# The embedding's products between the experts, a weight slot given up for their weights, and results added and normed by pairs of tiles

## What is computed

```python
x = x + merged @ w_o[i]
x = x + hierarchical_moe(rmsnorm(x, g_ffn[i]), ...)        # 32 experts, hidden 256, each token to 2 of them
ple_gate = sigmoid(rmsnorm(x, g_ple[i]) @ w_ple_gate[i])   # 1024 x 1024
x = x + (p[i] @ w_ple[i]) * ple_gate                       # p: 512 x 256, w_ple: 256 x 1024
```

## Time and profile before

| what | value |
|---|---|
| median of three runs | 2403.43 us |
| the profiled execution | 2404.18 us |
| its span in the trace | 2402.3 us |
| mean granted clock of TensorE | 0.988 |
| TensorE busy | 2278.5 us (95%) |
| VectorE busy | 999.4 us (42%) |
| ScalarE busy | 597.6 us (25%) |
| GpSimd busy | 409.7 us (17%) |
| SP's DMA queue, share of the 16 engines' span | 42.6% |

### The profile page before, as it was taken

One profiled execution on the slowest core, in us unless ns is written; L12 is line 12 of the kernel. 1 busy time (PEld: TensorE's weight loads), 2 busy tenths in 40 slices (PEclk: granted clock), 3 DMA queues, 4 the chain that ended last, 5 costly groups with the idle time before them and its releaser, 6 DMA issues. The chain is left out here.

```text
span 2402.3 us, 29837 instructions
## 1 busy us (share of the span) xinstructions
PE 2278.5 (95%) x11892; PEld 1695.5 (71%) x11892; DVE 999.4 (42%) x1787; ACT 597.6 (25%) x1245; POOL 409.7 (17%) x407
## 2 busy tenths in 40 slices
PE   8989999997899989999998889999989999999998
PEld 6666788654458767788754447877768887888887
DVE  6545533511145454543521136445743435232234
ACT  4523401311134443410311125233440003000012
POOL 2011111122211101111122221111101211111111
PEclk9999999999999999999999999999999999999999
DMA  5114536899962112234899982322213332333321
GB/s 172 44 55 107 132 106 261 320 422 422 420 251 61 58 38 70 58 105 164 332 420 422 422 342 64 104 80 86 80 38 101 92 119 73 103 97 97 97 97 71
DMA packets 291930, 396.57 MB, mean 165 GB/s; under 512 B 32590, under 2 KB 232014, under 8 KB 274378
## 3 DMA queue, kind: packets, MB, share of 16 engines
q1 hardware_dynamic: 274880, 366.27, 42.6%
q0 software_dynamic: 11328, 16.81, 1.9%
q10 hardware_dynamic: 5578, 11.51, 1.8%
HBM read 388.98 MB, written 30.15 MB: 174 GB/s over the span
## 5 line engine op out<-in xcount | busy, mean ns | idle before, releaser
L146 PE MATMUL banks<-h_split,w_high 128*128 128x512 f32 (+1 forms) x2640 | 826.8, 395 | 2.8 <-PEq L3441 1.7
L146 PEld LDWEIGHTS banks<-h_split,w_high 128*128 128x128 f32 x2640 | 482.8, 188 | 103.9 <-issue 8.2
L198 DVE TENSOR_TENSOR w_low<-w_raw,w_high 128x1024 fp32r<-128x1024 f32 (+1 forms) x264 | 317.1, 1201 | 506.8 <-POOL w_high L187 506.6
L187 POOL CAST w_high<-w_raw 128x1024 fp32r<-128x1024 f32 (+1 forms) x264 | 276.0, 1046 | 1441.5 <-PE banks L146 1307.3
L146 PE MATMUL banks<-h_split,w_low 128*128 128x512 f32 (+1 forms) x1320 | 513.4, 389 | 0.0
L146 PEld LDWEIGHTS banks<-h_split,w_low 128*128 128x128 f32 x1320 | 247.8, 188 | 52.4
L146 PE MATMUL banks<-w_high,op_split 128*128 128x512 f32 x736 | 228.5, 390 | 1.4 <-DVE mg_part L1420 1.1
L2154 PE MATMUL banks<-expert_ring,ex_xsT 128*64 128x256 f32 x1408 | 169.3, 395 | 29.4 <-DMA expert_ring<-in_w_exp_up 26.1
L2154 PEld LDWEIGHTS banks<-expert_ring,ex_xsT 128*64 128x64 f32 x1408 | 101.8, 142 | 84.6 <-DMA expert_ring<-in_w_exp_up 28.9
L146 PEld LDWEIGHTS banks<-w_high,op_split 128*128 128x128 f32 x736 | 138.1, 188 | 31.9 <-DVE mg_part L1420 2.4
L146 PE MATMUL banks<-w_low,op_split 128*128 128x512 f32 x368 | 143.2, 389 | 0.0
(11 more groups left out here) (444 smaller groups left out, 2738.1 us busy)
## 6 DMA issues: line engine op xcount, KB each, us to landing
w_raw<-in_w_in SPq DMA_DIRECT2D x142, 512.0 KB, 4.0
expert_ring<-in_w_exp_gate SPq DMA_DIRECT2D x42, 1024.0 KB
expert_ring<-in_w_exp_up SPq DMA_DIRECT2D x42, 1024.0 KB
expert_ring<-in_w_exp_down SPq DMA_DIRECT2D x42, 1024.0 KB
region<-in_w_exp_gate SPq DMA_DIRECT2D x22, 1024.0 KB
region<-in_w_exp_up SPq DMA_DIRECT2D x22, 1024.0 KB
region<-in_w_exp_down SPq DMA_DIRECT2D x22, 1024.0 KB
w_raw<-in_w_gu SPq DMA_DIRECT2D x44, 512.0 KB, 4.0
```

The costliest lines, as they stand in the source:

```text
L146: last = nc.tensor.matmul(out, left, right, start=(start and n == 0), stop=(stop and n == 2), skip_group_check=True)
L187: self.nc.gpsimd.tensor_copy(self.high[:, i % self.SPLIT, 0:n], self.raw[:, i % self.RAW, 0:n]).then_inc(self.high_ready, 1)
L198: self.nc.vector.tensor_tensor(self.low[:, i % self.SPLIT, 0:n], self.raw[:, i % self.RAW, 0:n], self.high[:, i % self.SPLIT, 0:n].bitcast ...
```

## The change

**Embedding's weights and products.** Slot 5 is used for the last time by expert 11. Behind the loads of expert 15 SP waits for block 11's down product and loads w_ple, 1 MB in one instruction, into the place of slot 5. The eight products stand on TensorE before gate and up of blocks 14, 16, 17, 19, 20, 21, 23 and 24, all into bank 7; ScalarE takes each out before the silu of the same block. The experts from 17 on use five slots by a table.

**Gate weights.** The loads of the first four pieces of w_ple_gate wait for 26 down products instead of 30, and their first three high parts are cast before the last but one scatter instead of behind the last.

**Results.** Tiles 0 and 1 are added, then the low copies of pair 0 are made, then tiles 2 and 3 and those of pair 1. TensorE transposes a pair (16 instructions), multiplies its two tiles by the first three pieces, then does the same for the other pair, and goes on as before.

**Order behind the gate product.** The squares go in the order HALVES, both sigmoids of tiles 0 and 1 stand ahead of their last squares, the half tile (3, 0) is squared behind the scaled rows of pair 0, and the first three pieces of the next stage are split inside this block, high parts and low parts, ahead of the last two and one of the gate's own.

**Start.** TensorE makes twelve products of 512 columns into bank 0, which nobody reads, before the tables' first products.

The diff without `SLOT_OF`'s uses in the loads and products, the functions moved from `LateNorm` to `Norm` as they are, and the waits that follow from HALVES:

```diff
 class FinalNorm / LateNorm
+HALVES = [(0, 0), (1, 0), (2, 0), (0, 1), (1, 1), (3, 0), (2, 1), (3, 1)]
...
 Tables.lines
+        pe.wait_ge(self.minus_ready, 2)
+        for _ in range(12):
+            self.nc.tensor.matmul(self.k.ps[:, 0, :].rearrange("p (n q) -> p n q", n=4), self.k.neg_ones[:],
+                                  self.k.neg_ones[:].unsqueeze(1).to_broadcast([P, 4, P]), start=True, stop=True)
...
 merge_and_route, SP
             for n in range(EXPERT_SLOTS + 2, EXPERTS):
                 e.load(sp, n)
-            for q in (e.pairs - 2, e.pairs - 1):
-                c = (q + 1) % GATHERS
-                sp.wait_ge(e.turned, 2 * q + 2)
-                sp.dma_start(*embedding.load_pair(c)).then_inc((p_landed0, p_landed1)[c], 16)
-            sp.wait_ge(e.down_done, EXPERTS - 2)
+                if n == SLOT_LEFT + 3:
+                    sp.wait_ge(e.down_done, SLOT_LEFT)
+                    embedding.load_weights(sp)
+            sp.wait_ge(e.down_done, e.order.index(GATE_RAW_AFTER) + 1)
             gate_stream.loads(sp, 0, gate_stream.RAW)
             e.stored(sp)
             results.load(sp)
...
 merge_and_route, POOL
-            e.pooled(pool, last_token, last_row, row_ready, refill_ready, last_weight_row)
+            def gate_highs(pool):
+                pool.wait_ge(e.down_done, e.order.index(GATE_HIGH_AFTER) + 1)
+                gate_stream.split_highs(pool, 0, gate_stream.SPLIT)
+
+            e.pooled(pool, last_token, last_row, row_ready, refill_ready, last_weight_row, gate_highs)
             e.scatter(pool, e.blocks - 1, last_row)
-            gate_stream.split_highs(pool, 0, gate_stream.SPLIT)
...
 merge_and_route, TensorE and ScalarE
-            e.multiply(pe, 2)
-            pe.wait_ge(p_landed0, 16)
-            pe.wait_ge(p_landed1, 16)
-            for i in range(EARLY_PRODUCTS):
-                wait(pe, embedding.ready, i - 1)
-                embedding.product(i, k.ps[:, i % 2, :]).then_inc(multiplied, 1)
+            e.multiply(pe, 2, embedding.product)
...
-            e.activate(act)
-            for i in range(EARLY_PRODUCTS):
-                act.wait_ge(multiplied, i + 1)
-                embedding.take(i, k.ps[:, i % 2, :])
+            e.activate(act, embedding.take)
...
+SLOT_OF = (*(n % 6 for n in range(17)), 0, 1, 2, 3, 4, 0, 1, 3, 4, 2, 0, 1, 3, 0, 1)
+SLOT_LEFT = 12
+GATE_RAW_AFTER, GATE_HIGH_AFTER = 25, 29
...
-EARLY_PRODUCTS = 4
+BETWEEN = (14, 16, 17, 19, 20, 21, 23, 24)
...
 class Experts
+    def slot(self, held):
+
+        return SLOT_OF[held] if self.refilled else held % len(self.slots)
+
+    def before(self, held):
+
+        return [n for n in range(held) if self.slot(n) == self.slot(held)]
+
+    def freed(self, sp, done, held):
+
+        if self.before(held):
+            sp.wait_ge(done, self.order.index(self.before(held)[-1]) + 1 if self.refilled else self.before(held)[-1] + 1)
...
-    def multiply(self, pe, start):
+    def multiply(self, pe, start, between=None):
         for n in range(start, self.blocks):
+            if between and n in BETWEEN:
+                between(pe, BETWEEN.index(n))
             self.gate_up(pe, n)
...
-    def activate(self, act):
+    def activate(self, act, between=None):
         for n in range(self.blocks):
+            if between and n in BETWEEN:
+                between(act, BETWEEN.index(n))
             self.silu(act, n)
...
 class Embedding
+        self.w = k.region[:, EXPERT_WORDS:EXPERT_WORDS + self.PC * D].rearrange("p (c n) -> p c n", c=self.PC)
+
+    def load_weights(self, sp):
+        sp.dma_start(self.w, self.w_ple.rearrange("(c p) n -> p c n", p=P)).then_inc(self.w_landed, 16)
...
 embed_per_layer, GpSimd
-        st.split_highs(pool, st.SPLIT, pieces)
-        pool.wait_ge(st.low_ready, pieces)
+        st.split_highs(pool, st.SPLIT, pieces - 2)
+        late.stream.split_highs(pool, 0, st.SPLIT)
+        st.split_highs(pool, pieces - 2, pieces)
...
 embed_per_layer, TensorE
-        for i in range(EARLY_PRODUCTS, 2 * NT):
-            wait(pe, embedding.ready, i - 1)
-            embedding.product(i, k.ps[:, i % 2, :]).then_inc(multiplied, 1)
-        for t in range(NT):
-            norm.open_tile(pe, t, (results.added, 2 * t + 2))
-        pe.wait_ge(embedding.ready, 2 * NT)
-        for e in range(pieces - st.SPLIT):
-            half = e // NT
+        early = 2 * st.SPLIT
+        for pair in range(PAIRS):
+            pe.wait_ge(results.added, 4 * pair + 4)
+            norm.turn_rows(pe, pair, k.x)
+            for c in range(early):
+                norm.pair_split(pe, pair, c)
+                st.rows(pe, c // 2, c % 2, 2, c, lambda t: k.ps[:, t, :], tiles=(2 * pair, 2 * pair + 1))
+        for c in range(early, DC):
+            norm.pair_split(pe, PAIRS - 1, c)
+            st.rows(pe, c // 2, c % 2, 2, c, lambda t: k.ps[:, t, :])
+        for e in range(NT, pieces - st.SPLIT):
             for n in (0, 1):
...
 embed_per_layer, ScalarE
         for t in range(NT):
-            norm.high(act, 2 * t)
-            norm.high(act, 2 * t + 1)
+            if t % 2 == 0:
+                for c in range(DC):
+                    norm.high_pair(act, t // 2, c)
             nc.scalar.activation(junk[:, t * D:(t + 1) * D], k.x[:, t, :], ACT.Square, accum_out=norm.ss[:, t:t + 1]).then_inc(norm.squares_done, 1)
...
-        for t in range(NT):
+        for t in (0, 1, 2):
             late.square(act, t, 0)
         for t in (0, 1):
             gate(NT + t)
+        for t in (0, 1):
             late.square(act, t, 1)
         gate(NT + 2)
         act.preload_act_table_set("sqrt_and_others")
         late.root(act, 0)
         late.odd_tile(act, 0)
+        late.square(act, 3, 0)
         late.square(act, 2, 1)
...
 embed_per_layer, VectorE
         for t in range(NT):
             results.add(k, dve, gate, t)
-        dve.wait_ge(norm.gain_landed, 16)
-        for step in "h0 h1 h2 h3 h4 w3 h5 h6 h7".split():
-            (norm.low if step[0] == "h" else st.split_low)(dve, int(step[1]))
+            if t % 2:
+                dve.wait_ge(norm.gain_landed, 16)
+                for c in range(DC):
+                    norm.low_pair(dve, t // 2, c)
+        st.split_low(dve, 3)
         norm.following_vector(dve)
-        for i in (4, 5, 6):
+        for i in (4, 5):
             st.split_low(dve, i)
-        for t in range(NT):
+        for i in range(st.SPLIT):
+            late.stream.split_low(dve, i)
+        st.split_low(dve, 6)
+        for t in (0, 1, 2):
...
```

More of the change, by code:

```diff
@@ L298, in scale @@
         self.nc.scalar.activation(x, x, ACT.Copy, scale=self.ss[:, t:t + 1]).then_inc(done, 1)
+PAIRS, PAIR = NT // 2, 2 * P
 class Norm:
+    places = tuple(tuple((bank + c // 2, c % 2 * PAIR) for c in range(DC)) for bank in (2, 4))
     def __init__(self, k, ctx, tag, gain, banks, xn, follows=False, small=None):
@@ L2071, in refill_down @@
     def refill_down(self, pool, last_row):
-        _, down = self.slots[RESIDENT % len(self.slots)]
+        _, down = self.slots[self.slot(RESIDENT)]
         pool.wait_ge(self.down_done, RESIDENT + 1)
@@ L2077, in load_gate_up @@
     def load_gate_up(self, sp, n, expert):
[L2078 to L2081 removed]
+        u = self.slot(n)
+        self.freed(sp, self.gu_done, n)
+        for dst, src in expert_parts(self.slots[u], *(w[self.layer, expert] for w in self.weights))[0:2]:
+            sp.dma_start(dst, src).then_inc(self.w_landed[u], 16)
     def load_down(self, sp, n, expert):
[L2084 to L2087 removed]
+        u = self.slot(n)
+        self.freed(sp, self.down_done, n)
+        dst, src = expert_parts(self.slots[u], *(w[self.layer, expert] for w in self.weights))[2]
+        sp.dma_start(dst, src).then_inc(self.down_landed[u], 16)
     def load(self, sp, n):
@@ L2130, in pooled @@
                 self.refill_down(pool, last_weight_row[1])
+            if ahead and n == self.blocks - 2:
+                ahead(pool)
             self.scatter(pool, n, last_row)
@@ L2166, in down @@
     def down(self, pe, n):
-        U, held = len(self.slots), self.held(n)
-        pe.wait_ge(self.down_landed[held % U], 16 * (held // U + 1))
+        held = self.held(n)
+        u = self.slot(held)
+        pe.wait_ge(self.down_landed[u], 16 * (len(self.before(held)) + 1))
         if self.refilled and self.order[n] == EXPERTS:
@@ L2431, in vector @@
             late.follow(dve, t, 0)
+        gated(3)
         for t in (0, 1):
             gated(NT + t)
-            late.follow(dve, t, 1)
+        for t, half in ((0, 1), (1, 1), (3, 0)):
+            late.follow(dve, t, half)
         late.sums(dve, 0)
-        late.stream.split_low(dve, 0)
         gated(NT + 2)
```

124 lines of the change are left out of this document (53 added, 71 removed).

## The result

| | kernel before | changed kernel |
|---|---|---|
| median of 8 runs each | 2404.34 us | 2411.43 us |
| ratio, 95% interval | 1 | 1.0027 (1.0018 to 1.0036) |
| the profiled execution | 2404.18 us | 2408.84 us |
| its span | 2402.3 us | 2407.1 us |
| mean granted clock | 0.988 | 0.980 |

The change makes the kernel 7 us slower. Run once more beside the experiments it was at 1.0018 (1.0009 to 1.0027), so 4 to 7 us. The forecast was 2399.8 us, with 2391.5 to 2407.5 as its range: wrong in sign.

A forecast was written before the change was run, and what follows sets the result against it. TensorE was taken as busy nearly all the time, with DMA setting the pace in part of the experts. Terms -0.4 - 0.6 + 1.7 - 4.3 = -3.6 took 2403.4 to 2399.8 us; range 2391.5 to 2407.5.

The forecast's parts named there:

- The experts' part: Products between experts: TensorE waits 12.4 us before expert 14, experts end 1.8 us later in layer 0, 4.0 in layer 1.
- Rival C: Experts: the products' weights come late, 6 us more per layer, 2411.8 us in all; chance 0.13.
- the closing norm's order: Behind layer 1's gate product: first product 2.9 us sooner, no half clock and transposes 1.4 more, -4.3 us; layer 0 nothing.
- The further 1.4 us for full clock behind it: Layer 1, behind the closing norm: no half clock at the product's start (1.3 us), some 1.4 with the transposes.
- The last scatter: End of layer 0's experts: casts ahead make block 31's scatter 2 us later, the last (684) hardly; nothing.
- g_ple as the bound: Ahead of the gate product: the scale vector's landing holds the first scaled copy; first product 1.6 us behind that copy.
- rival B: Ahead of the gate product: the scale vector doesn't hold the first pair, additions decide; 2391.8 us in all; chance 0.19.
- The forecast's 1.7 us for the gate product of layer 0: Layer 0's gate product: TensorE, idle for 14 us before, no longer at full clock, costs 1.7 us.
- rival D: Nothing measurable: half clock lasts twice as long at four places and in the closing norm's wait; 2402 to 2406; chance 0.21.
- Rival B's sum: Layer 0's first gate product if additions decide: 697 + 1.8 + 2.8, given as 701.2 us at worst.
- The start: Twelve products at the kernel's start: transposes at full clock take 1.95 instead of 3.00 us; gain 0.4 us, between 0 and 0.9.

The follow-up runs named there:

- e5: Changed kernel with the eight products before blocks 17, 18, 19, 20, 22, 24, 25 and 26; ratio 1.0018 to the kernel before.
- e2: Changed kernel with the next stage's first three pieces split where the kernel before splits them, behind the gate's own; ratio 1.0000 to the kernel before.
- e8: Kernel before with only the order of squares and sigmoids behind the gate product changed, next stage's splits left in place; ratio 0.9995 to the kernel before.
- e1: Changed kernel with the three casts of the gate's weights put back behind the last scatter; ratio 1.0009 to the kernel before.
- e4: Changed kernel with g_ple (4 KB) loaded ahead of the wait for the last scatters, so ahead of the results; ratio 1.0003 to the kernel before.
- e7: Kernel before with only the experts' part: w_ple in slot 5's place, products between experts, five slots, gate's raw weights as changed; ratio 1.0033 to the kernel before.

## Why the prediction was wrong

**The experts' part was sized right.** The weights landed 1 to 2 us sooner than computed, counted from the first expert. In the eight profiles with products at the change's places the experts take 235.3 and 235.5 us on average, in the five without 232.3 and 232.8: +3.0 and +2.75, together 5.75 where the forecast had 1.8 + 4.0 = 5.8. That is 2.75 us for one more megabyte, the pace of the earlier trace rows; in e5's one profile (234.1 and 237.2) another place of the products changes nothing. The forecast's two shares (1.8 and 4.0) don't show, and single profiles of one layer differ by up to 3.9 us. The Trainium skill's rule (DMA: Bandwidth & Descriptors, Queues, rings and completion order) that descriptors are consumed in ring order holds here: the megabyte came at 546.2, not at 534.6. Rival C, which had the right time (2411.8), had it by a transfer 6 us later than this; it isn't what happened.

**The step that failed is the closing norm's order**, where the forecast wrote that "VectorE is free of two splits" and counted only what that brings. Left out, and so put at nothing, was what stands behind the moved splits in the lists: the gate's own last two pieces. TensorE waits for their low parts in both gate products (0.9 to 1.6 and 2.5 us). These products took 47.4 and 53.0 us in one profile and 49.2 and 50.4 in the other, against 47.4 and 47.5 in the forecast. Putting the splits back gave 4 to 6.5 us (e2), of which the profiles at full clock show 3.3. That 47.4 of the first profile meets the forecast is luck: the forecast had 1.7 us of half clock in it, but full clock was back at 703.4, before the product, and waits stood in its place. Also put at nothing was the wait of GpSimd that the change drops: by the traces it is behind the 1.37 us that stay in e2, which no run with the line put back has tested.

The norm itself went as forecast in kind: 0.51 us of waiting for the scaled rows, 2.05 for the copies. Its first product came 3.9 us sooner behind the gate product where the forecast had 2.9: 2.3 for the order (e8), 0.6 for the splits (e2), and 1.0 for casts that no longer run beside VectorE there, which the forecast hadn't counted. The further 1.4 us for full clock behind it don't show: from this product to the end of the span it is 904.4 us in both kernels.

**The last scatter** was said to go "hardly" later. It goes 2.3 us later behind the last down product in layer 0 and 1.5 in layer 1, as the casts in front of it wait for raw weights that come behind the last expert's. In the second profile it is 1.3 and 0.7 us. e1 has 2 to 4 us less time, within the noise.

**g_ple as the bound** was right: first product 1.5 us behind its landing (703.62 against 702.12), and rival B's gain appears where the load is moved (e4).

**The clock.** The forecast's 1.7 us for the gate product of layer 0 is in e7 (1.75), but not in the changed kernel's first profile, as said. In layer 1 it took the price as paid already (1.6 us, 47.3 against 45.7). The changed kernel's profile had half clock until 1450.9, 5.8 us into the product, which costs 2.9 us, 1.3 more; the second until 1448.8, 3.2 us in, which costs 1.6, no more than before; e2's only until 1443.5, which costs nothing. A part of rival D is so in the result, with a size that moves from run to run.

**Rival B's sum** has a slip: 697 + 1.8 + 2.8 is 701.6, not 701.2, which is not ahead of the forecast's 701.4. Nothing in the result hangs on it.

**The start** gave nothing: first product at 13.26 and 12.68 us against 12.99. The timeline of the changed kernel's start shows why:

```profile
1.40 5.49 PE L637 MATMUL banks<-neg_ones 128*128 128x512 f32 x12 [1.40 <-POOL neg_ones L622]
...
10.17 3.44 PE L326 MATMUL banks<-identity,region 128*128 128x128 f32 x16 [1.08 <-DVE region L484]
```

Where the sum went wrong can be taken by stretch, both layers together: the forecast (from its 682.7 and 701.4, 1423.4 and 1443.6, 47.4 and 47.5, and 5.6 for the norm), then the two profiles of the changed kernel.

| stretch | forecast | first profile | second |
|---|---|---|---|
| experts | 470.3 | 468.4 | 470.9 |
| to the gate product | 39.0 | 41.5 | 39.7 |
| gate products | 94.9 | 100.4 | 99.5 |
| to the next product | 8.1 | 6.7 | 6.7 |

The gate products are 4.6 to 5.5 us too long, and nothing else is off by as much. All four are 4.7 us over the forecast in the first profile and 4.5 in the second. With 0.4 for the start and 1.4 for the clock behind the norm, neither of which came, -3.6 becomes +2.7 to +2.9 us. The second profile is 2.7 us longer than the kernel before (span 2405.0); the first is 4.8 longer, of which 2.0 stand ahead of the first expert. The medians are 4.4 and 7.1 us over; what they have beyond the profiles was not taken apart.

## What to carry to other kernels

Work moved ahead in an engine's list is paid by what stands behind it there: find in each list the next item that a bound engine waits for, and what the moved item itself waits for. In this kernel a transfer in a stretch where the DMA engines are full cost its own time, at either place of its consumer. A wait that looks needless can keep two engines out of each other's way: look at what will run at the same time when it is gone. What looks like spare work on the bound engine (products in a wait) can be what keeps its clock up and fits the wait: measure how many fit before moving them away.

## What the hardware showed

TensorE's clock came back at different times behind similar waits of 15 to 17 us: after the first pair's transposes in layer 1 half clock lasted to 1450.9, 1448.8, 1446.0, 1443.5 and 1442.5 in five profiles whose transposes all started between 1439.6 and 1440.4. And twelve products of 0.46 us each at the start, ended 3.3 us before the transposes, did not save these from half clock: sixteen took 3.4 and 2.8 us in the two profiles of the changed kernel, 3.0 in the kernel before without them, and 1.95 at full clock.

VectorE's operations with two inputs ran slower beside a cast on GpSimd: 1.4 to 1.5 us instead of 0.7 for a product or addition of 128x512, 2.05 instead of 1.22 for a split of 128x1024 (e2 against e8).
